# Expert rows weighed on ScalarE and turned by adding transposes, in place of products with diagonal blocks

## What is computed

```python
def peer_ffn(h, w_query, sub_keys, expert_u, expert_v):
    ...
    experts = jnp.take_along_axis(cand_i, best_pos, axis=-1).reshape(T, PEER_HEADS * PEER_TOPK)
    gates = jax.nn.softmax(best_s, axis=-1).reshape(T, PEER_HEADS * PEER_TOPK)
    def expert_block(args):
        tb, eb, gb = args
        act = jax.nn.gelu(jnp.einsum('td,ted->te', tb, expert_u[eb]).astype(jnp.float32), approximate=False)
        return jnp.einsum('te,ted->td', (gb * act).astype(tb.dtype), expert_v[eb])
```

## Time and profile before

| | |
|---|---|
| median of 3 runs | 2707.04 us (2697.24 to 2708.9) |
| span of the profiled execution | 2613.3 us |
| runs' median over that span | 93.7 us |
| busy: PE, PE weight load | 2263.2 us (87%), 2100.8 us |
| busy: DVE, ACT, POOL | 1559.2 us (60%), 455.3 us (17%), 1185.7 us |
| moved by DMA | 901 MB, 345 GB/s over the span |
| of these gathered rows (POOL's queue) | 537 MB |

### The profile page before, as it was taken

One profiled execution on the slowest core, in us unless ns is written; L12 is line 12 of the kernel. 1 busy time (PEld: TensorE's weight loads), 2 busy tenths in 40 slices (PEclk: granted clock), 3 DMA queues, 4 the chain that ended last, 5 costly groups with the idle time before them and its releaser, 6 DMA issues. The chain is left out here.

```text
span 2613.3 us, 41465 instructions
## 1 busy us (share of the span) xinstructions
PE 2263.2 (87%) x16702; PEld 2100.8 (80%) x16702; DVE 1559.2 (60%) x4047; ACT 455.3 (17%) x985; POOL 1185.7 (45%) x1030
## 2 busy tenths in 40 slices
PE   8987889878879877788987888887889889999999
PEld 6886689778768877777887876887858888899799
DVE  1248577776867868857777687785877632311310
ACT  1210233001023110113301222100221011201200
POOL 0026656777757768766676643544434400000000
PEclk9998989978999988898998887989888899999999
DMA  8479999999999999999999977899978968468374
GB/s 314 152 297 402 414 384 356 412 409 410 408 413 392 412 413 411 405 414 386 362 403 411 404 304 277 339 417 416 368 275 316 418 243 362 166 240 319 133 267 150
DMA packets 179327, 901.15 MB, mean 345 GB/s; under 512 B 20765, under 2 KB 23873, under 8 KB 155969
## 3 DMA queue, kind: packets, MB, share of 16 engines
q0 software_dynamic: 147632, 537.47, 52.7%
q1 hardware_dynamic: 30400, 357.95, 34.7%
q10 hardware_dynamic: 1104, 3.08, 0.3%
HBM read 897.37 MB, written 1.05 MB: 344 GB/s over the span
## 5 line engine op out<-in xcount | busy, mean ns | idle before, releaser
L2231 POOL DMA_INDIRECT urow<-in_expert_u,idx x512 | 604.0, 1180 | 641.2 <-DVE dots L1846 351.5
L787 PE MATMUL ea<-diag,vrow 128*128 128x128 f32 x4176 | 558.1, 300 | 192.1 <-DMA vrow<-in_expert_v,idx 192.1
L787 PEld LDWEIGHTS ea<-diag,vrow 128*128 128x128 f32 x4176 | 544.8, 215 | 207.2 <-issue 207.2
L2231 POOL DMA_INDIRECT vrow<-in_expert_v,idx x512 | 580.0, 1133 | 255.0 <-issue 148.1
L1846 DVE CUSTOM_DVE_ANT_0 urow<-urow,h2n 128x1024 f32<-128x1024 f32 x512 | 601.0, 1221 | 25.4 <-DMA urow<-in_expert_u,idx 24.2
L1834 DVE SCALAR_TENSOR_TENSOR acc<-vrow,wgt,acc 128x1024 f32<-128x1024 f32 x247 | 317.2, 1284 | 152.8 <-DMA vrow<-in_expert_v,idx 141.2
L860 PE MATMUL ea<-hB,wring 128*128 128x144 f32 (+1 forms) x1120 | 157.9, 306 | 33.4 <-DMA wring<-in_weights 14.6
L860 PEld LDWEIGHTS ea<-hB,wring 128*128 128x128 f32 x1120 | 154.1, 210 | 37.1 <-issue 21.3
L860 PE MATMUL pa<-hB,wring 128*128 128x144 f32 (+1 forms) x992 | 131.7, 296 | 14.5 <-DMA wring<-in_weights 14.5
L860 PEld LDWEIGHTS pa<-hB,wring 128*128 128x128 f32 x992 | 129.3, 202 | 15.5 <-DMA wring<-in_weights 15.3
L1342 ACT ACTIVATE gl<-dots 128x4 f32<-128x4 f32 x128 | 26.3, 205 | 651.9 <-DVE dots L1846 651.3
(11 more groups left out here) (509 smaller groups left out, 3140.2 us busy)
## 6 DMA issues: line engine op xcount, KB each, us to landing
wring<-in_weights SPq DMA_DIRECT2D x95, 2048.0 KB, 10.5
wlate<-in_weights SPq DMA_DIRECT2D x25, 2048.0 KB, 8.4
w<-in_weights SPq DMA_DIRECT2D x24, 2048.0 KB, 10.6
wring<-in_weights SPq DMA_DIRECT2D x22, 1408.0 KB, 7.0
wlate<-in_weights SPq DMA_DIRECT2D x10, 1408.0 KB, 6.6
urow<-in_expert_u,idx POOLq DMA_INDIRECT x512, 11.5
vrow<-in_expert_v,idx POOLq DMA_INDIRECT x512, 12.4
wring<-in_weights SPq DMA_DIRECT2D x3, 1792.0 KB, 9.8
```

Of the source, the lines that this page charges most:

```text
L787: m = pe.matmul(EA[c // 4][:, (c % 4) * P:(c % 4 + 1) * P], vrow[:, b, c * P:(c + 1) * P], diag[:, DIAG_SLOTS * (q % 2) + i, :], start=Fal ...
L2231: pool.indirect_dma_start(out=rows[:, b, :], out_offset=None, in_=table, in_offset=bass.IndirectOffsetOnAxis(ap=idx[:, k % 2, col:col + 1] ...
```

## The change

ScalarE weighs three gathered v rows of each group in place (`scale_rows`), in its own order right after the Gelu of the next group. PE then takes each of their eight column blocks as stationary operand and the plain identity as moving one, with the transpose mode on, and adds the result into the same PSUM banks. The diagonal blocks and their buffer are gone, and with them DVE's wait for their use by PE; a semaphore `weighted` stands where a settle stood behind the weights, and `scaled` counts the weighed rows. The nine `DENSE` groups a tile now have three rows on PE like the others.

```diff
-DENSE = (0, 1, 5, 6, 7, 21, 22, 25, 30)
-def summed(q):
-    return SUMMED[q // GROUPS_TILE] + (q // GROUPS_TILE < UNITS - 1 and (q - 1) % GROUPS_TILE in DENSE)
-PE_ROWS = [GB - summed(q) for q in range(UNITS * GROUPS_TILE)]
-DIAG_SLOTS = max(PE_ROWS)
+PE_ROWS = [GB - SUMMED[q // GROUPS_TILE] for q in range(UNITS * GROUPS_TILE)]
...
-            diag = sb("diag", [P, 2 * DIAG_SLOTS, P])
...
                     for i in range(PE_ROWS[q]):
                         b = GB * (g % 2) + i
-                        pe.wait_ge(diag_done, pe_rows(q) + i + 1)
-                        pe.wait_ge(v_full[b], 16 * (q // 2 + 1))
+                        pe.wait_ge(scaled, pe_rows(q) + i + 1)
                         for c in range(KC):
-                            m = pe.matmul(EA[c // 4][:, (c % 4) * P:(c % 4 + 1) * P], vrow[:, b, c * P:(c + 1) * P],
-                                          diag[:, DIAG_SLOTS * (q % 2) + i, :], start=False, stop=False)
+                            m = pe.matmul(EA[c // 4][:, (c % 4) * P:(c % 4 + 1) * P], vrow[:, b, c * P:(c + 1) * P], ident,
+                                          start=False, stop=False, is_transpose=True)
                         m.then_inc(v_free, 1)
...
+            def scale_rows(q):
+                if PE_ROWS[q]:
+                    act.wait_ge(weighted, q + 1)
+                for i in range(PE_ROWS[q]):
+                    b = GB * (q % 2) + i
+                    act.wait_ge(v_full[b], 16 * (q // 2 + 1))
+                    act.activation(vrow[:, b, :], vrow[:, b, :], ACT.Copy, scale=wgt[:, q % 2, i:i + 1]).then_inc(scaled, 1)
...
                         act.activation(gl[:, g % 2, :], dots[:, g % 2, :], ACT.Gelu).then_inc(gelu_done, 1)
+                        if k * GROUPS + g:
+                            scale_rows(k * GROUPS + g - 1)
...
             def sum_rows(q, first, last):
+                dve.wait_ge(weighted, q + 1)
...
                     if q >= 2:
-                        dve.wait_ge(diag_done, pe_rows(q - 1))
-                    estep(tt_(wgt[:, g % 2, :], gl[:, g % 2, :], gates[:, GB * g:GB * g + GB], ALU.mult))
-                    esettle()
-                    if q >= 2 and PE_ROWS[q]:
-                        dve.wait_ge(v_free, rows_used(q - 1))
-                    for i in range(PE_ROWS[q]):
-                        dve.tensor_scalar(diag[:, DIAG_SLOTS * (q % 2) + i, :], ident, wgt[:, q % 2, i:i + 1], None, ALU.mult)\
-                           .then_inc(diag_done, 1)
+                        dve.wait_ge(scaled, pe_rows(q - 1))
+                    tt_(wgt[:, g % 2, :], gl[:, g % 2, :], gates[:, GB * g:GB * g + GB], ALU.mult).then_inc(weighted, 1)
```

More of the change, by code:

```diff
@@ L393, in program @@
         gelu_done, gate_exp, e_acc = sem("gelu_done"), sem("gate_exp"), sem("e_acc")
-        diag_done, e_step, e_gmax, e_idx, e_key, e_x = (sem(n) for n in (
-            "diag_done", "e_step", "e_gmax", "e_idx", "e_key", "e_x"))
+        weighted, scaled, e_step, e_gmax, e_idx, e_key, e_x = (sem(n) for n in (
+            "weighted", "scaled", "e_step", "e_gmax", "e_idx", "e_key", "e_x"))
         w_full = [sem(f"w_full{i}") for i in range(RING + LATE)]
```

## The result

The changed kernel takes **2870.01 us** (median of 4 runs, 2856.41 to 2875.26) where the kernel before takes 2707.97 (2697.24 to 2709.45): ratio **1.061** [1.057, 1.065], slower by 162 us. The forecast was 2733, the range 2690 to 2785: the direction was right, the amount far outside.

What follows compares the result with a forecast made beforehand. The stage was taken as bound by DMA bytes, with PE setting the pace in the attention loops. Loop +12, output projections +9 and clock +5 gave +26 us on 2707: 2733 us, slower by 1.0%, range 2690 to 2785.

Steps and rivals of the forecast that it cites:

- What bounds the stage: Stage from 183 to 1471 us: bound by its bytes, so relief of an engine can return at most 31 us.
- The new wait: Attention loop: PE's rows wait for weighing behind the next group's dots and Gelu, adding 2.1 us a slot in window 1.
- the DMA has a backlog to work off: Slots 19 to 21 and after: backlog absorbs most of 13 us delay; 3 us a window taken, +9 us.
- No cost of its own: GpSimd and SP: v buffers and weight tiles come free later, but this adds nothing beyond delays already counted.
- halving the term of window 2: Window 2's loop: the DMA needs 12.8 us a slot, over the 11.9 taken, so 3.6 of 7.2 us counted.
- The loop's term: Attention loop, slots 8 to 15: three slots pay in full, one by 0.6 us; 17.4 - 5.4 = +12 us.
- The clock: PE's waits in loop slots lower its granted clock: one slow slot a window, +5 us, bounds 0 and 36.
- rival C: PE granted 1.2 GHz much of the time, under 0.9 in the loops: 63 us less a third, 2775 us; chance 0.18.
- A: Rival: added delays vanish in the DMA's backlog over the stage, 2707 us, between 2700 and 2718; chance 0.22.
- B: Rival: PE's relief closes the gaps in the loops and part of the rest, 22 us faster, 2685 us; chance 0.15.
- The base: Whole kernel: forecast starts from median 2707; its 93.7 us above the 2613.3 span taken as work around the instructions.
- the last link: Loop slot, first weighed row to next scores: two more weighings and eight transposes, forecast at 3.15 us.

Runs made afterwards that it cites:

- the better order: The changed kernel with ScalarE weighing ahead of the Gelu, except in groups 10 to 12 of each tile: 2593.42 us, ratio to before 0.9936.
- the wait alone: The kernel before, with PE's rows of each group held until the next group's Gelu is done, nothing else changed: 2809.16 us, ratio 1.0758.
- the pair of traces: Traces of the kernel before, span 2613.3 us, and of the unaltered changed kernel run again on an experiment chip, span 2728.3 us.
- The filler: The changed kernel with 16 products of zeros added on PE ahead of each group's rows: 2704.36 us, ratio to before 1.035.
- the changed kernel's repeat: The changed kernel, unaltered, run again on a chip used for the experiments: 2730.34 us, ratio to the kernel before 1.045.
- its twin with products: The changed kernel with transpose mode off, so plain products by the identity, in the same order: 2978.33 us, ratio to before 1.1405.

## Why the prediction was right in direction and wrong in amount

**What bounds the stage: right.** With PE relieved and nothing held back the kernel before gives 0.9939 and the better order 0.9936, some 16 us each, of the 31 that I named as the most to be had.

**The new wait: right in mechanism.** All links could be read from the trace before the change, three of four to within 0.4 us. The first transpose waits for ACT, the wait alone costs 200 us, and undoing the order undoes the loss.

**The step that failed is "this stretch is at 398 GB/s and the next at 411: the DMA has a backlog to work off".** I priced slots 17 to 24 between 0 and 13 us a window and took 3; measured, 18.5 a window in the pair of traces (55.5 in three), and the kernel that is late there, otherwise in the better order, takes 58 us more. The term was short by 46.5 us, half of the 89 by which the whole sum was short of the 115. A share of 1.01 says that the DMA was never without work while everything went at its pace. It doesn't say that work lies ahead. What is asked for is set by `u_free`, in step with DVE's dots, and DVE stood in the very chain that was made longer. My 14.7 MB "allowed in flight" were allowed and not queued. The same step is the fault in "No cost of its own" for GpSimd, whose wait for PE's rows went from 8.9 us to 76.6, and in halving the term of window 2, whose slots 13 to 15 lose 3.1 to 4.5 us each. Even my upper bound of 13, nothing absorbed, was short of 18.5: from the first weighing to the last transpose slot 19 takes 6.6 us (513.52 to 520.08, below), where I had 4.25.

**The loop's term: the size was off, +45 for +12.** Two causes. A slot lost 3.8 us and not 2.1, since I had ScalarE pace the turning, with the transposes at full speed, and PE paced it at half for most of it (below). And the slots, from first dot to first dot over three windows: slots 12 to 15 lose 6.5, 9.7, 11.0 and 11.1 us, 38 together, where my three full slots and the partial one made 17.4. Slots 8 to 11 lose 9 in all (+21, -13, +4 and -4), where I had set a gain of 5.4, and slot 16 gains 2. With only groups 9 to 16 late, slot 8 takes 42.3 us, no more than in the better order: its loss comes from the groups ahead of the loop. In that kernel slots 12 to 15 alone lose 50 us against the better order, four slots a window at 4.2 each. So the number of slots that pay was nearly right, and each pays about twice what I had.

**Slots 0 to 7: left out, +14.5.** There the same chain runs beside the projections, and I priced it at nothing.

**The clock: the size was off, at least 26 us for 5.** The filler gives 26 us back, inside the bounds of 0 to 36, where I had put one slow slot a window. The granted clock of the loop was 0.87, under the 0.9 that I had named as rival C's sign, and C would still have been the wrong account: most of the loss stays with the clock at 0.93. Of the 63 us that it priced the clock at, 26 are shown, with a loss beside them over three times as large.

**The rivals.** A, the delays vanish in the backlog, is the failed step at its full size and false. B, PE's relief closes the gaps, is true once the chain is gone: I gave 22 us for it and 16 were measured; in the changed kernel its condition, dots done before PE wants the rows, isn't met, as I held: PE waits 4.20 us for ScalarE in the slot above.

**The base: wrong, and harmless here.** I took the 93.7 us between the median and the span for work around the instructions. The profiled execution of the changed kernel took 2856.41 us with a span of 2854.5: 1.9 us lie around it. So the trace of before, with a span of 2613.3, came from a faster execution than the runs shown beside it.

## What to carry to other kernels

When an engine gets new work for a consumer, ask first what stands ahead of it in that engine's own order: here the same 1.1 us instruction costs 118 us in all behind a Gelu that needs the next group's dots, and ahead of it the kernel takes the time of before. A DMA share near 1 is no reserve; look at what each transfer's issue waits for, and if that is the delayed chain, count the delay in full. And choose the order slot by slot: neither one, taken everywhere, was the best.

## What the runs showed of the hardware

**Transposes and the clock.** Behind a long wait PE turns rows at half clock for some microseconds; it doesn't take products to end that. Timeline of slots 19 and 20 of the changed kernel's repeat, then windows: the transposes of the loop slot above, whole and in two parts, and those of slot 19 and across their end:

```profile
499.88 7.46 PE L607 MATMUL pa<-ydT,w 128*128 128x128 f32 x64
...
513.52 3.21 ACT L1330 ACTIVATE vrow<-vrow,wgt 128x1024 f32<-128x1024 f32 x3
...
514.70 5.38 PE L776 MATMUL ea<-kst,vrow 128*128 128x128 f32 x24 [7.36 <-ACT vrow L1330]
```

```profile
438.40:443.00 4.60, 4.53 (x25) 4.37 (x25) 0.65 (x2) 3.38 (x4) 3.02 (x3) 0.63 0.73 210
...
438.80:442.10 3.30, 3.30 (x17) 3.30 (x16) 0.25 (x2) 2.98 (x3) 2.69 (x3) 0.50 0.80 209
442.20:442.90 0.70, 0.70 (x7) 0.54 (x5) 0.00 (x0) 0.00 (x0) 0.08 (x1) 1.00 0.77 293
...
514.70:517.20 2.50, 2.50 (x12) 2.50 (x13) 0.00 (x0) 2.48 (x3) 1.89 (x3) 0.50 0.44 116
517.20:519.80 2.60, 2.60 (x14) 2.60 (x13) 0.00 (x0) 2.34 (x3) 1.60 (x2) 0.50 1.01 370
519.90:522.00 2.10, 2.10 (x17) 2.10 (x17) 0.00 (x0) 0.00 (x0) 1.34 (x2) 0.82 0.86 304
522.00:524.00 2.00, 2.00 (x20) 2.00 (x20) 0.00 (x0) 0.00 (x0) 1.48 (x2) 1.00 0.97 342
```

The clock of the loop slot's turning was 0.63: that is the last link's 4.4 us. In slot 19 24 transposes in a row take 5.38 us at a granted 0.50 (1.2 GHz), 0.224 us each, with no idle time between them, and the products behind them have it at 1.00 within 2.1 us. In the loop slot the clock falls just behind the start of the turning, after the wait of 4.20 us, and is back at 1.00 from 442.2 on, though PE has run nothing but transposes since 438.47. This is no rarity: in 44 of the 96 groups of the repeat the clock comes back in the midst of the turning, behind a wait of over 1 us and with no other work of PE between. The medians of the weight loads over the stage differ between the repeat and its twin with products (230 ns and 192, the shortest 137 and 186):

```profile
L776 PEld LDWEIGHTS ea<-kst,vrow x2304: 137/230/231, 204.7 to 1602.8; 128*128 128x128 f32 x192
```

```profile
L776 PEld LDWEIGHTS ea<-kst,vrow x4608: 186/192/339, 204.0 to 1854.9; 128*128 128x128 f32 x192
```

More than half of the transposes run at the slow level, and more than half of the products at the full one. But that is no sign that transposes hold the clock down: by the granted clock at each record the twin spends 344 us of its rows at half clock and the repeat 297, and it is the products that are more in number and last longer. The rule that the prediction cited (the Trainium skill, "TensorE: Matmul & The Clock Gate", Part 4: PE-mode transpose) says that transpose-mode work is not counted as PE being busy in the same way and that the full clock doesn't engage for it. This trace doesn't agree: with f32 transposes alone the clock rises. Nor are transposes always slow: in the better order 24 of them, from 384.4 us, take 3.17 us at a granted 1.00, ScalarE's pace, with products ahead of them and a wait of only 1.5 us.

**ScalarE.** 128x1024 in place with a scale column takes 1.135 us as a record, and 3.21 for three in a row, so (3.21 - 1.135)/2 = 1.04 apart. The estimate from narrower ones was 1.12.

**Unlike times of one kernel.** The kernel before takes 2708 us in the first runs and 2608 to 2612 on the three chips of the experiments, and the changed one 2870 and 2730. The ratio moves too, 1.061 and 1.045. In the first execution of the changed kernel some slots are longer without another wait for an engine; 64 records of products from 638.24 us to 649.58, with pauses in the issue between them, take 11.3 us in place of 7.3:

```profile
645.90 0.99 PE L607 MATMUL pa<-logit_exp,wring 128*128 128x128 f32 x5 [0.64 <-issue]
...
648.77 0.81 PE L607 MATMUL pa<-logit_exp,wring 128*128 128x128 f32 x3 [0.72 <-issue]
```

Over that execution such pauses of PE add up to 61.5 us, and to 0.4 in the repeat. What makes them is open: the traces of the changed kernel's variants have no more of them than the repeat, so they could not be tested.
